# V tiles of a PEER retrieval layer: two blocks of 512 columns in two column groups, or four blocks of 256 in four

## What is computed

```python
def peer(h, wq, subkeys, u, v):          # D_MODEL 1024, PEER_CHUNK 128 tokens, 8 chunks
    ...                                  # 8 heads x 16 best keys = 128 indices a token
    g = jax.nn.softmax(top_s, axis=-1)
    act = jax.nn.gelu(jnp.einsum('nhkd,nd->nhk', u[idx], xc))
    return jnp.einsum('nhk,nhkd->nd', g * act, v[idx])
```

## Time and profile before

| | |
|---|---|
| median of 3 runs | 3441.04 us |
| lowest, highest | 3435.26, 3443.61 us |
| span of the profiled execution | 3447.3 us (no other time of it is given; 6.3 us or 0.18% above the median) |
| PE, DVE, ACT, POOL busy | 72%, 59%, 23%, 61% of the span |
| V matmuls (L2100) | 4096 records, 4 for each of 1024 tiles |
| HBM traffic | 1148.13 MB read, 13.63 MB written, 337 GB/s over the span |

### The profile page before, as it was taken

The page is one execution under the profiler, slowest core; times in us unless marked ns, Lnnn a source line. Parts: engine busy times, 40 slices in busy tenths (PEclk is TensorE's granted clock), DMA queues, the critical chain, the costliest instruction groups (busy, mean ns, idle before and its releaser), DMA issues.

```text
span 3447.3 us, 29321 instructions
## 1 busy us (share of the span) xinstructions
PE 2466.8 (72%) x9222; PEld 1078.6 (31%) x9222; DVE 2047.0 (59%) x4621; ACT 785.3 (23%) x1888; POOL 2087.7 (61%) x2167
## 2 busy tenths in 40 slices
PE   7978977768676776677777867787767766533476
PEld 4844654324221432134222422143213422000011
DVE  4785786666655666656656566665665666565300
ACT  2265111122112221222122221222122212100121
POOL 6910254566666666666666666666666666666665
PEclk8989987886789667865797578956796688855699
DMA  8533499799999999999999999999999999999998
GB/s 319 179 140 113 142 337 358 288 358 362 349 371 367 360 364 367 362 368 358 364 367 375 361 364 372 372 358 366 364 361 370 361 355 359 372 379 368 364 367 323
DMA packets 335937, 1163.76 MB, mean 338 GB/s; under 512 B 40485, under 2 KB 51365, under 8 KB 333608
## 3 DMA queue, kind: packets, MB, share of 16 engines
q0 software_dynamic: 297792, 1084.36, 83.6%
q1 hardware_dynamic: 37994, 77.54, 6.3%
HBM read 1148.13 MB, written 13.63 MB: 337 GB/s over the span
## 4 chain that ended last, share of the span: by engine, by line
PE 29%; POOL 16%; issue 14%; another core or an unknown queue 13%; DMA 12%; DVE 11%; ACT 4%; SPq 1%; DVEq 0%; ACTq 0%; POOLq 0%
POOL arena L619 16%; DMA arena<-in_v,arena 9%; PE psum L2100 9%; DVE arena L1565 6%; PE psum L1931 4%; PE psum L1899 4%; DMA arena<-in_u,idx_u 2%; PE psum L2034 2%; PE psum L1920 2%; PE psum L1946 2%; PE psum L1781 1%; PE psum L1956 1%; PE psum L1980 1%; ACT arena L883 1%
## 5 line engine op out<-in xcount | busy, mean ns | idle before, releaser
L1565 DVE CUSTOM_DVE_ANT_0 arena<-arena,psum 128x1024 f32<-128x1024 f32 x1024 | 1215.6, 1218 | 413.3 <-DMA arena<-in_u,idx_u 379.4
L619 POOL DMA_INDIRECT arena<-in_u,idx_u x1024 | 960.0, 937 | 652.8 <-issue 267.8
L2100 PE MATMUL psum<-arena 128*32 128x512 f32 x4096 | 1013.0, 744 | 445.6 <-DMA arena<-in_v,arena 305.4
L619 POOL DMA_INDIRECT arena<-in_v,arena x1024 | 977.6, 955 | 522.1 <-issue 256.8
L2100 PEld LDWEIGHTS psum<-arena 128*32 128x32 f32 x4096 | 181.8, 124 | 1185.3 <-issue 1036.6
L960 ACT ACTIVATE arena<-arena 128x32 f32<-128x32 f32 x1024 | 277.6, 314 | 1166.4 <-PE psum L2100 580.1
L1899 PE MATMUL psum<-kT,arena 64*128 64x512 f32 (+1 forms) x384 | 252.4, 810 | 56.2 <-issue 26.9
L1920 PE MATMUL psum<-ident,arena 128*128 128x128 f32 x560 | 137.5, 378 | 174.5 <-issue 110.3
L1401 DVE TENSOR_REDUCE small<-psum 128x1 f32<-128x1280 f32 x64 | 95.4, 1491 | 278.4 <-remote 220.8
L1931 PE MATMUL psum<-v,arena 128*128 128x64 f32 x1120 | 230.4, 395 | 27.3 <-ACT arena L883 24.0
L2034 PE MATMUL psum<-wbig,arena 128*128 128x512 f32 x512 | 242.4, 628 | 4.5 <-issue 3.4
(11 more groups left out here) (268 smaller groups left out, 2154.9 us busy)
## 6 DMA issues: line engine op xcount, KB each, us to landing
arena<-in_u,idx_u POOLq DMA_INDIRECT x1024
arena<-in_v,arena POOLq DMA_INDIRECT x1024
arena<-in_w_mod POOLq DMA_DIRECT2D x20, 512.0 KB, 4.3
wbig<-in_wq SPq DMA_DIRECT2D x1, 7168.0 KB, 19.7
arena<-in_w_mod SPq DMA_DIRECT2D x12, 512.0 KB, 4.1
arena<-in_xin SPq DMA_DIRECT2D x5, 1024.0 KB, 9.6
arena<-in_w_mod SPq DMA_DIRECT2D x2, 2048.0 KB, 10.7
wbig<-in_w_mod SPq DMA_DIRECT2D x2, 2048.0 KB, 20.5
```

Of the source, the lines that this page charges most:

```text
L619: pool.indirect_dma_start(ring[:, r, :], None, t[table], bass.IndirectOffsetOnAxis(idx[:, j:j + 1], 0)).then_inc(got[r], 16)
L1565: V.tensor_tensor_reduce(ring[:, r, :], ring[:, r, :], hx_cur, 1.0, 0.0, ALU.mult, ALU.add, act_[:, j:j + 1]).then_inc(S["u_used"], 1)
L2100: ins = M(bank(4 + b)[QP * g:QP * g + QP, :], lhsT=sel[:, j % SELS, :], rhs=ring[:, r, 512 * b:512 * b + 512], start=(i == 0), stop=(i == ...
```

## The change

A V tile is multiplied in four calls of 256 columns, each in a column group of its own (group q XOR b for block b), where there were two calls of 512 columns. Blocks 0 and 1 lie in bank 4, blocks 2 and 3 in bank 5. As two blocks now share a bank and a column group, only the first matmul issued into each pair of bank and group has the start flag. `move_sum` then has to put blocks right that stand turned by one, two or three groups: 11 copies of 256 columns in place of 3 of 512.

```diff
             def move_sum(c):
                 act.wait_ge(S["v_used"], (c + 1) * SLOTS)
                 act.wait_ge(S["ff_free"], c + 1)
-                A(ff[:, 0:512], bank(4), ACT.Copy)
-                A(ff[0:64, 512:D], bank(5)[64:P, :], ACT.Copy)
-                A(ff[64:P, 512:D], bank(5)[0:64, :], ACT.Copy).then_inc(S["ffn_out"], 1)
+                A(ff[:, 0:256], bank(4)[:, 0:256], ACT.Copy)
+                for q in range(2):
+                    A(ff[64 * q:64 * q + 64, 512:768], bank(5)[64 - 64 * q:P - 64 * q, 0:256], ACT.Copy)
+                for b in (1, 3):
+                    for q in range(QUADS):
+                        g = QP * (q ^ b)
+                        ins = A(ff[QP * q:QP * q + QP, 256 * b:256 * b + 256],
+                                bank(4, 2)[g:g + QP, 256 * b:256 * b + 256], ACT.Copy)
+                ins.then_inc(S["ffn_out"], 1)
...
-                    for b in range(2):
-                        g = (q + 2 * b) % QUADS
-                        ins = M(bank(4 + b)[QP * g:QP * g + QP, :], lhsT=sel[:, j % SELS, :],
-                                rhs=ring[:, r, 512 * b:512 * b + 512], start=(i == 0), stop=(i == QP - 1))
+                    for b in range(4):
+                        g = q ^ b
+                        ins = M(bank(4, 2)[QP * g:QP * g + QP, 256 * b:256 * b + 256], lhsT=sel[:, j % SELS, :],
+                                rhs=ring[:, r, 256 * b:256 * b + 256], start=(i == 0 and q % 2 == 0), stop=(i == QP - 1 and q % 2 == 1))
                     ins.then_inc(S["v_used"], 1)
```

## The result

| | before | changed |
|---|---|---|
| median of 4 runs each, side by side | 3438.15 us | 3510.07 us |
| lowest, highest | 3433.21, 3443.61 | 3508.37, 3516.91 |
| ratio, 95% interval | | 1.0197 [1.017, 1.0223] |

The change makes the kernel 2% slower, 72 us by the medians. The profiled execution took 3509.82 us.

The account below looks back on a forecast made before the run. The prediction took the DMA engines, busy 0.97 over 2782 us, as the bound. Launch end +2, seven chunk turns +8 and V tiles among attention -11 gave -1 us: 3441 - 1 = 3440 us, range 3421 to 3459.

Parts of the forecast that it names:

- Data come at 1.24 us a tile at best, so I cost the loads at nothing: TensorE's V tiles: eight weight loads instead of four, some 0.44 us in a queued tile's 0.43 us period, priced at zero.
- A V tile: On TensorE, a lone tile would take 0.62 us at clock 1.00 and 1.07 us at 0.50; queued tiles no faster.
- The rival that they would not: Only two groups run side by side inside one tile, which stays at 1.05 us: 3461 us, chance 0.05.
- The copies: In move_sum, 11 copies of 256 columns take 4.3 us instead of 1.80 us for three: 2.5 us more.
- Turns and end: Seven chunk turns lose 1.2 us each, 8 us in all; the launch's end is 2.1 us longer.
- the 5 I named for it: At a chunk's turn, the gather behind it would wait about 5 us in place of 3.5.
- The mixed stretch: Where V tiles run among attention work, earlier tile ends would return buffers sooner and gain 11 us.
- My key: V tiles' 46% of POOL's waits for consumers gives them 23 of some 50 DMA holes, each regaining 0.5 us.
- "mixed stretch decides" rival: TensorE's chain among attention shortens by 60 us, 35 us of it from DMA holes: 3416 us, chance 0.22.
- The clock: Rival: shorter busy time lowers TensorE's clock, other matmul work grows, 15 us of it through holes: 3454 us, chance 0.08.
- The test that I set: Wrong if DMA share moves over 0.005 (14 us): upwards, TensorE's lateness made the holes; downwards, turns or clock did.
- The highest of my rivals: Slowest alternative: tile stays at 1.05 us, each turn costs 2.5 us more: 3461 us, chance 0.05.

Follow-up runs that it names:

- the eight waits: Kernel before, with eight waits for the same already met semaphore ahead of each V tile instead of one: 1.0003 in fast memory, 1.0086 (33 us) in slow memory.
- the last series: Slow memory, kernel before 3442.09 us: four 256-column calls with three copies, in two column groups 3482.44 us (1.0089), in four groups 3488.27 us (1.0143).
- the three-copy kernel: Changed matmuls, four calls in four groups, with the three copies of the kernel before: 3562.42 us, 1.0267, in the slowest memory, where before took 3467 us.
- the run with 128 columns: Changed kernel's instructions with calls of 128 columns in four groups, three copies, half the columns left out, against the kernel before: 1.0001 in fast memory.

## Why the prediction was wrong

**The step that failed** is "Data come at 1.24 us a tile at best, so I cost the loads at nothing". It put at nothing all that twice the calls and loads might cost on TensorE. I compared the loads' busy time, 0.44 us, with the tile's period and found room on the mean; the price of the further instructions had no other term. Cutting each call in two, in the column groups of before, cost 45 us in one series of slow memory (1.0129 [1.0103, 1.0155]) and 31 us in another (1.0089 [1.0058, 1.0121]; 40 us by the medians), and nothing that could be told in fast memory, twice. That it costs nothing in fast memory doesn't clear TensorE's own time: the eight waits do take such time, and behave the same way. Why it costs what it does in slow memory stays open.

**What the 72 us are made of.** In the series with all parts but one, the doubled instructions give 45 us (3484.41 - 3439.14) and the rest of the change 25 us more (3509.0 - 3484.41). The copies are 13 of these (8 by the medians), by the kernel with them alone, in another series; 12 to 17 us are left for the four groups side by side. In the last series these groups give 6 us by the medians and 0.5% or 18 us by the ratios, whose intervals overlap. That they add something of their own, some 6 to 18 us, is likely but not shown. The 93 us of the three-copy kernel in the slowest memory show that all such sums hold for one state of the memory only.

**What is shown and what is argued.** Shown: cutting the calls in two costs most of the time, in slow memory alone. Two things come with it there: the spells of steps of 0.71 us, and more of the late signals with a hole behind each. Not shown is what makes either. Two findings speak against the theory that the spells are TensorE's wait for code. In the changed kernel no packet of the instruction queue is on its way in the last spell (3485.30 to 3491.01 us): the launch's last one began at 3483.82 and took 0.92 us. And the packets come no slower than in fast memory: the median of one is 0.947 us in the changed kernel's profile of slow memory and 0.936 in that of fast. In all, 14 of the 303 us of spells have such a packet on its way. What stands of the theory is that 8192 further instructions are 32 further packets, 256 a packet. The cost is not in proportion to the count either: 33 us for 4096 instructions of waiting, 31 to 45 for 8192 of matmul and weight load. Three rivals are left untested: that it is the weight loads and not the count; that it depends on how long a call is (the run with 128 columns met fast memory); and that it is the recording of each instruction, since no execution timed here is without a span and a granted clock on record.

The Trainium skill ("Runtime: NRT & Kernel Launch", Instruction fetch mechanics) says that an engine's sequencer fetches its code in blocks of 256 instructions by a DMA queue of its own, and that crossing a block is mostly hidden. The trace agrees on the 256 (8192 instructions, 32 packets), and in fast memory nothing speaks against the hiding; in slow memory the packets' times don't show it failing.

**The other steps, in their order.**

- *A V tile*: I said 0.62 and 1.07 us; the rows show 0.64 and 1.08, and 8192 records. The four blocks do lie side by side (the first four matmuls of a tile enter within 0.02 us, at 3484.14). The rival that they would not has fallen.
- *The copies*: I said 4.3 us; it is 4.25 (0.38 + 0.77 + 3.08 and pauses), and pieces of 32 partitions cost what those of 128 do.
- *Turns and end*: I said 10 us; 13 [4, 22] were measured. The first V matmul of the turn is later by 2.46 us, as I had it. The gather behind the turn shown waited 3.09 us, not the 5 I named for it; where the turn's loss lies is not shown.
- *The mixed stretch*: I said 11 us gained; half the columns at the instructions of before gained 9 us at most, with whatever the lower clock cost already taken off. My key, 23 holes by 0.5 us, has nothing measured behind it, and no run shows a gain like that of the "mixed stretch decides" rival (35 us in the holes). The key also took the holes as of one kind; in the changed kernel the four largest but for the start are those behind a late signal, which a shorter V tile doesn't touch.
- *The clock*: its fall is real. The lead at 2554 us stands at 0.81 where the earlier trace rows have 0.93, with the same columns multiplied; the mixed stretch shown above keeps its 0.70. But the price of 15 us is not borne out: half the columns at 0.667 lost nothing on balance, and the whole change at 0.749 loses next to nothing in fast memory. In slow memory its price alone was not measured.
- *The test that I set*: the DMA share moved by more than 0.005, downwards, to 0.95. I had put down only turns or clock for that sign. The turns are 8 to 13 us of it; for the larger part no rival of mine had the mechanism. The highest of my rivals was 3461 us, against 3510 measured.

## What to carry to other kernels

Give the number of instructions a term of its own, with a range, when a split gives an engine the same work in more calls: a mean rate that leaves room is no reason for nothing. Cut the calls without the rest of the change and measure that alone. When a profile shows an odd pattern, such as the steps of 0.71 us, look whether the bounding resource is idle beside it before calling it the cause; here it was busy. Look then at its largest holes, and compare when a producer's record ends with when its consumer starts. Time a change under both rates of memory if they occur: 2% here was next to nothing there.

## What the hardware showed that I had not expected

- The same kernel took 3082 us or 3438 to 3467 us, by the rate at which the gathers came (419 or some 365 GB/s), and one chip showed both.
- TensorE's records come in steps of 0.71 us for microseconds on end, with half a V tile (four matmuls, four loads) in two steps, then seven tiles in 4.85 us.
- ScalarE starts 0.04 us after the last transpose's recorded end in fast memory, in every chunk; in slow memory it starts 15 to 19 us after it in 26 of 84 cases, and was idle for 11 us or more of that.
- In fast memory the mean granted clock of the whole kernel fell from 0.85 (two groups) to 0.75 with four groups side by side, and to 0.65 with calls of 128 columns (half of the columns left out), with no effect on the time.
- A copy of 32 partitions by 256 columns out of PSUM takes 0.374 us, one of 128 partitions 0.383.
